# A two-block network on one Trainium2 core: first operand without its root mean square, filter spectrum beside the first product, modulation products moved later

## The chip, the cores and the metric

One core of a Trainium2 chip runs the whole program in one launch. The metric is device time in microseconds (us) for one execution; lower is better. Engines: PE (TensorE), DVE (VectorE), ACT (ScalarE), POOL (GpSimd), and SP, whose queue issues the weight transfers.

## The reference

Two blocks on x (256 rows of 2048 numbers), all in f32. What matters here, cut:

```python
h = rms_norm(x, norm_mix_g)           # x * rsqrt(mean(x*x) + eps) * g
u = h @ w_in                          # 2048 -> 2576 (SSD) + 3520 (RWKV)
x = x + concat([ssd_mixer(u[:, :2576]), rwkv7_mixer(u[:, 2576:])]) @ w_out
x = x + memory_cross_attention(rms_norm(x, g), rms_norm(mem, g), wq, wk, wv, wo)
x = x + square(relu(rms_norm(x, g) @ ffn_w1)) @ ffn_w2
# second block
mod = silu(c) @ ada_w + ada_b         # 2048 -> 12288: shift, scale, gate, twice
mod_c = silu(c_ctx) @ ada_w + ada_b
h, hc = modulate(rmsnorm(x, norm1_g), sh1, sc1), modulate(rmsnorm(ctx, norm1_g), csh1, csc1)
q, k, v, f, hy = split(h @ w_in_2);  kc, vc = split(hc @ w_in_2[:, 1024:3072])
y = merge_groups(attention(q, k, v, kc, vc), fourier_mix(f), hyena_mix(hy, filter_spectrum))
x = x + g1 * (y @ w_out_2)
x = x + g2 * conv_gated_mlp(modulate(rmsnorm(x, norm2_g), sh2, sc2))
return rmsnorm(x, final_norm_g)
```

The filter spectrum is computed from small weights alone (two layers with sine, a third layer, a window, a Fourier transform). The modulation `mod` needs only c, c_ctx and ada_w.

## The kernel before

Activations lie by features: 16 tiles of 128 features by 256 positions. Each weight product is near-f32: a weight chunk of 512 KB lands in one of six buffers (`wraw`), ACT copies it to rounded form (`split_hi`, line 516, tile `whi`), DVE subtracts to get the rest (`split_lo`, line 523, `wlo`); there are four buffers of each. The operand is split in the same way (HH, HL). Each chunk of `gemm_p` is 24 matmuls (lines 566, 568, 569): high by high, high by low, low by high.

The program runs products in a written order: ada0, in_ssd, in_rwkv, xk, xv, out, xq, xo, four times up and dn, ada3, then those of the second block. Every engine walks the same list by itself. SP issues the chunks in that order (`sync`, line 2484), a chunk at a time, each after its buffer is free: a split chunk's buffer is free after `split_lo`, an ada chunk's only after its matmuls on PE. ACT splits three chunks ahead of PE, DVE two.

Beside a product lies other work, cut into steps. `Side.beside(product, every)` lets one step of the side follow each product chunk, more or fewer by `every`; the side's waits stand in the engine's own order, so PE stands still at a side step whose input is late. `weave` puts two steps of an extra product after every `per` steps of the main one.

The modulation product is 24 pieces of 512 columns (`ada_p`, line 692: 16 f32 matmuls in four groups at four column positions of the array; `gather`, line 676, adds the four partial sums; ACT copies PSUM to `mo`, DVE adds the bias into MOD). A piece is 8 chunks, not split. Pieces 0 to 5 are ada0, at the start of the program; 6 to 11 are ada1, woven into xk and xv; pieces 12 and later come in the second block.

Beside ada0 run, one after another: the norm of x (squares on ACT, sums on POOL, matmuls with ones at line 794, square root, reciprocal, x times g and 1/rms on DVE at line 833, high and low split), then the filters' spectrum (lines 930 to 1005), which ends with a store to DRAM that POOL issues and waits for. in_ssd starts after the last MOD of ada0. Its tiles are copied out of PSUM by ACT, with Silu for the first eight (line 1010), those of in_rwkv too (line 1023). Beside in_rwkv runs the SSD mixer, first 12 steps of convolution on DVE (lines 1034, 1037), and later the norm of mem, whose 1/rms is applied after the products xk and xv. Beside xk and xv, and on into out, runs the RWKV mixer, in two halves.

Of the kernel before, what the change touches and what calls it, by code (L numbers as in the profile page):

```python
# [17 lines left out]
NA0 = 6  # L18
WK = 2
WV = 4  # L20
# [3 lines left out]
NA1 = 9  # L24
# [120 lines left out]
def idle(n):  # L145
    for _ in range(n):
        yield
# [39 lines left out]
def build(nc, A_, out):  # L187
    top = ExitStack()
    with top:
# [6 lines left out]
        def landing(name):  # L196
            return count(name, 16)
# [32 lines left out]

        sx, new = scope()
        X0 = new("x0", [P, 16, T])
        TM1 = new("tm1", [P, 8, T])
        RS1 = new("rs1", [P, T])
        sp, new = scope()
        SPEC0 = new("spec", [P, 2, 2, 2, 512])
# [6 lines left out]
        HF = new("hf", [P, 2, 2048])  # L243
        HD = new("hd", [64, 3, T])
        sp.close()
        sx.close()

        rk, new = scope("right")
        RK = new("rk", [P, 28, T + 1])
        sb, new = scope()  # L250
        ZZ = new("zz", [P, 8, T])
        XB = new("xb", [P, 12, T + 3])
        DT = new("dt", [16, 4, T])
# [54 lines left out]
        SMX = new("sm4", [P, 8, 4])  # L308
        s5, new = scope()
# [83 lines left out]
        d_pk, d_mt, d_x0, d_m1, d_sel = (landing(n) for n in ("pk", "mt", "x0", "m1", "sel"))  # L393
# [49 lines left out]
        made(plan_ada("ada0", 0, NA0))  # L443
        made(plan("in_ssd", "w_in", 0, 16, cols(0, 2560) + [(2560, 128)], "a"))
        made(plan("in_rwkv", "w_in", 0, 16, cols(2576, 5648, 256) + [(5648, 224), (5840, 256)], "a"))
        woven = plan_ada("ada1", NA0, NA2)
# [5 lines left out]
        made(plan("xo", "xattn_wo", 0, 16, cols(0, 2048, 256), "v", 2))  # L452
        for i in range(4):
            made(plan(f"up{i}", "ffn_w1", 0, 16, cols(2048 * i, 2048 * i + 2048, 256), "v"))
            made(plan(f"dn{i}", "ffn_w2", 16 * i, 16, cols(0, 2048, 256), "v"))
# [213 lines left out]
        def ada_bank(n):  # L669
            return (1 if NA0 <= n < NA2 else 0) + 2 * (n % 2)  # L670

# [172 lines left out]
        def mem_a(e):  # L844
            e.wait_ge(*d_mem.at("all"))
            e.activation(TM2[:, 0:4, :], MX[:, 0:4, :], ACT.Square).then_inc(*mem.a.up(("sq", 0)))
            yield
            for g in range(1, 4):
                if g > 1:
                    e.wait_ge(*mem.g.at("sum", g - 1))  # L850
                e.activation(TM2[:, 4:8, :], MX[:, 4 * g:4 * g + 4, :], ACT.Square).then_inc(*mem.a.up(("sq", g)))
                yield
                yield
            e.wait_ge(*mem.p.at("ss"))
            e.activation(RS2, PSUM[:, 4, 0:T], ACT.Sqrt, bias=col("eps6"), scale=1.0 / 2048)
            e.activation(RC2[:, :], PSUM[:, 5, 0:4], ACT.Sqrt, bias=col("eps6"), scale=1.0 / 2048).then_inc(*mem.a.up("rt"))
            yield

        def mem_g(e):
            for g in range(1, 4):  # L860
                e.wait_ge(*mem.a.at("sq", g))
                if g > 1:
                    e.wait_ge(*mem.g.now())
                e.tensor_tensor(TM2[:, 0:4, :], TM2[:, 0:4, :], TM2[:, 4:8, :], ADD).then_inc(*mem.g.up(("sum", g)))

        def mem_p(e):
            yield from idle(7)
            e.wait_ge(*ssd.a.end())
            e.wait_ge(*ssd.v.end())
            e.wait_ge(*mem.g.at("sum", 3))  # L870
            for i in range(4):
                e.matmul(PSUM[:, 4, 0:T], ones, TM2[:, i, :], start=i == 0, stop=i == 3)
            for r in range(2):
                for i in range(4):
                    x = e.matmul(PSUM[:, 5, 2 * r:2 * r + 2], TM2[:, i, 128 * r:128 * r + 128], ones[:, 0:2], start=i == 0, stop=i == 3)
            x.then_inc(*mem.p.up("ss"))
            yield

        def mem_v(e):
            yield from idle(7)  # L880
            e.wait_ge(*mem.a.at("rt"))
            e.reciprocal(RS2, RS2)
            e.reciprocal(RC2[:, :], RC2[:, :]).then_inc(*mem.v.up("rs"))
            yield
# [14 lines left out]
        def spectrum_g(e):  # L899
# [6 lines left out]
            yield  # L906
            yield
            yield
            for n in range(4):
                yield  # L910
            for o in range(2):
# [3 lines left out]
                yield  # L915
                yield
                yield
# [92 lines left out]
        def ssd_evac_a(e, g, q, t, what):  # L1010
            e.wait_ge(*mm.at("tile", g, q))
            ps = tile_of(g, q)
            if t < 8:
                x = e.activation(ZZ[:, t, :], ps, ACT.Silu)
            elif t < 20:
                x = e.activation(XB[:, t - 8, 3:T + 3], ps, ACT.Copy)
            else:
                x = e.activation(DT[:, 0, :], ps[0:16, :], ACT.Copy)
            x.then_inc(*ev_a.up((what, g), ("ssd", t)))

        def rwkv_evac_a(e, g, q, t, what):
            e.wait_ge(*mm.at("tile", g, q))
            e.activation(U(t), tile_of(g, q), ACT.Copy).then_inc(*ev_a.up((what, g), ("rwkv", t)))
# [3 lines left out]
        def ssd_v(e):  # L1027
            e.wait_ge(*ev_a.at("ssd", 20))
# [82 lines left out]
            e.wait_ge(*ssd.v.now())  # L1111
            e.tensor_tensor(YS[:, :, :], YS[:, :, :], ZZ[:, :, :], MUL).then_inc(*ssd.v.up("gated"))
# [10 lines left out]
        def ssd_a(e):  # L1123
# [41 lines left out]
            for g in range(2):  # L1165
# [5 lines left out]
                yield  # L1171

# [139 lines left out]
        def mixing_g(e):  # L1312
            e.tensor_tensor(M1C[:, 1:10, 0:64], M1C[:, 1:10, 0:64], M1C[:, 1:10, 64:128], ADD).then_inc(*rw.g.up())
            e.tensor_tensor(M1C[:, 0, 0:64], ident[:, 0:64], ident[:, 64:128], ADD).then_inc(*rw.g.up("masks"))
            for n in range(14):
                e.wait_ge(*ev_a.at("rwkv", 2 * n + 1))
# [1173 lines left out]
        def tensor(e):  # L2490
            e.wait_ge(*d_mt.at("all"))
            side = Side(idle(5), norm_p(e, fn, TM1), spectrum_p(e))
            side.beside(ada_p(e, "ada0", MO0[:, :]))
            side.rest()
            first = lambda e, k: e.wait_ge(*fn.v.at("lo", k // 4))
            e.wait_ge(*ada.v.at("mod", NA0 - 1))
            for _ in gemm_p(e, PL["in_ssd"], [(HH, HL)], first):
                pass
            e.wait_ge(*spt.a.end())
            side = Side(ssd_p(e), idle(1), mem_p(e), idle(12))  # L2500
# [9 lines left out]
            e.wait_ge(*ada.v.at("mod", NA2 - 1))  # L2510
# [15 lines left out]
            side = Side(idle(6), norm_p(e, ctx, TM, lambda e: e.wait_ge(*res.a.at("rt", "xo"))))  # L2526
            for i in range(4):
                side.beside(gemm_wide_p(e, PL[f"up{i}"], GX, lambda e, k: None if i else e.wait_ge(*res.v.at("lo", "xo", k)),
                                        (lambda e, ci: ci == 3 and factor_p(e, "xo", ACC[:, :])) if i == 0 else None))
                side.beside(gemm_wide_p(e, PL[f"dn{i}"], HX, lambda e, k: e.wait_ge(*ff1.v.at("lo", i, k))))  # L2530
# [49 lines left out]
        def vector(e):  # L2580
            ada_first_v(e)
            lo_to = Ahead(split_lo)
            side = Side(idle(5), norm_v(e, fn, X0, TM1, RS1[:, :], HH, HL, lambda j: col("norm_mix_g", j), None), spectrum_v(e))
            side.beside(ada_v(e, "ada0", lo_to))
# [435 lines left out]
```

## Time and profile before

| what | value |
|---|---|
| median of three runs (lowest, highest) | 3333.25 us (3332.19, 3339.2) |
| the profiled execution: its time, its span | 3332.07 us, 3330.2 us |
| mean granted PE clock | 0.965 |
| PE busy, share of span | 3135.5 us, 94% |
| DVE busy | 1870.8 us, 56% |
| ACT busy | 1403.3 us, 42% |
| POOL busy | 240.3 us, 7% |
| HBM read | 591.34 MB, 180 GB/s over the span |

Times in the rows are us from the start of the span unless marked ns. A number in brackets behind a row is the time for which its engine stood idle just before, and what ended that. A granted clock of 1.00 is 2.4 GHz on PE, 0.5 is 1.2 GHz. f32 matmuls appear as two records each.

### The profile page before, as it was taken

How to read it: one execution, taken by the hardware profiler on the slowest of the kernel's cores; microseconds unless marked ns; L12 is line 12 of the kernel's file. 1: busy time of each engine (PE TensorE's matmuls, PEld its weight loads, DVE VectorE, ACT ScalarE, POOL GpSimd, SP SyncE). 2: the span in 40 equal slices, each digit the busy share in tenths (PEclk: the TensorE clock that was granted, in tenths of full speed). 3: DMA queues.
4: the chain of work that ended last, by engine and by line, in shares of the span. 5: the costliest groups of instructions: out<-in, count | busy, mean ns of one | idle time of the engine just before them, and what ended most of it. 6: DMA issues, size and time to landing. Idle time of an engine off the chain costs nothing.

```text
span 3330.2 us, 53960 instructions
## 1 busy us (share of the span) xinstructions
PE 3135.5 (94%) x22542; PEld 2708.2 (81%) x22542; DVE 1870.8 (56%) x2505; ACT 1403.3 (42%) x1992; POOL 240.3 (7%) x204
## 2 busy tenths in 40 slices
PE   6799998989999999999999989999888999999998
PEld 1599897879788888888888769988466888888887
DVE  2247575373655676665656632254445666666666
ACT  1245352253443465444545432344234544445443
POOL 1000122011000110000000300010001000000002
PEclk7899999999999999999999979999988999999999
DMA  8665454555654566565656562445856566656654
GB/s 297 222 177 159 133 179 164 182 168 163 225 161 131 157 203 197 183 194 181 195 185 189 172 203 89 124 143 164 283 177 219 181 185 190 188 176 195 192 178 143
DMA packets 518452, 603.26 MB, mean 181 GB/s; under 512 B 18890, under 2 KB 442981, under 8 KB 516720
## 3 DMA queue, kind: packets, MB, share of 16 engines
q1 hardware_dynamic: 510112, 569.73, 54.6%
q0 software_dynamic: 3488, 25.88, 2.1%
q10 hardware_dynamic: 4608, 4.20, 0.4%
q8 instruction: 178, 2.92, 0.4%
q14 instruction: 66, 0.54, 0.1%
HBM read 591.34 MB, written 8.39 MB: 180 GB/s over the span
## 4 chain that ended last, share of the span: by engine, by line
PE 76%; DVE 4%; issue 4%; DMA 2%; ACT 2%; POOL 1%; SPq 0%; DVEq 0%; ACTq 0%; POOLq 0%
PE psum L594 34%; PE psum L595 18%; PE psum L566 3%; PE psum L568 3%; PE psum L569 3%; PE psum L1725 2%; PE psum L628 2%; PE psum L692 2%; PE psum L631 1%; PE psum L630 1%; DVE wlo L523 1%; PE psum L676 1%; PE psum L2379 1%; DMA wraw<-in_ada_w 1%; PE psum L2137 0%
## 5 line engine op out<-in xcount | busy, mean ns | idle before, releaser
L523 DVE TENSOR_TENSOR wlo<-wraw,whi 128x1024 fp32r<-128x1024 f32 (+2 forms) x916 | 1109.8, 1221 | 561.5 <-ACT whi L516 559.6
L516 ACT ACTIVATE whi<-wraw 128x1024 fp32r<-128x1024 f32 (+2 forms) x916 | 944.8, 1033 | 1078.6 <-PE psum L595 713.2
L594 PE MATMUL psum<-g,whi 128*128 128x512 f32 x2944 | 1045.3, 397 | 1.7 <-DVE wlo L523 1.1
L595 PE MATMUL psum<-g,wlo 128*128 128x256 f32 x2944 | 825.6, 280 | 0.0
L594 PE MATMUL psum<-h,whi 128*128 128x512 f32 x2240 | 791.4, 395 | 6.0 <-DVE wlo L523 5.7
L594 PEld LDWEIGHTS psum<-g,whi 128*128 128x128 f32 x2944 | 556.1, 189 | 136.2 <-DVE wlo L523 2.6
L595 PE MATMUL psum<-h,wlo 128*128 128x256 f32 x2240 | 634.8, 283 | 0.0
L595 PEld LDWEIGHTS psum<-g,wlo 128*128 128x128 f32 x2944 | 556.2, 189 | 0.5
L594 PEld LDWEIGHTS psum<-h,whi 128*128 128x128 f32 x2240 | 422.2, 188 | 103.8 <-DVE wlo L523 6.1
L595 PEld LDWEIGHTS psum<-h,wlo 128*128 128x128 f32 x2240 | 422.8, 189 | 0.1
L566 PE MATMUL psum<-h,whi 128*128 128x256 f32 x1040 | 303.6, 292 | 13.3 <-DVE wlo L523 10.8
L568 PE MATMUL psum<-h,whi 128*128 128x256 f32 x1040 | 297.6, 286 | 0.0
L569 PE MATMUL psum<-h,wlo 128*128 128x256 f32 x1040 | 297.3, 286 | 0.0
L566 PEld LDWEIGHTS psum<-h,whi 128*128 128x128 f32 x1040 | 201.2, 193 | 27.0 <-DVE wlo L523 14.2
L568 PEld LDWEIGHTS psum<-h,whi 128*128 128x128 f32 x1040 | 201.4, 194 | 0.4 <-issue 0.2
L569 PEld LDWEIGHTS psum<-h,wlo 128*128 128x128 f32 x1040 | 200.9, 193 | 0.0
L692 PE MATMUL psum<-wraw,sf 128*32 128x512 f32 x768 | 131.7, 776 | 47.2 <-DMA wraw<-in_ada_w 43.1
L566 PE MATMUL psum<-g,whi 128*128 128x256 f32 x512 | 153.5, 300 | 0.4 <-issue 0.4
L569 PE MATMUL psum<-g,wlo 128*128 128x256 f32 x512 | 145.1, 283 | 0.0
L568 PE MATMUL psum<-g,whi 128*128 128x256 f32 x512 | 145.0, 283 | 0.0
L1840 DVE TENSOR_TENSOR xt<-psum,xt 128x256 f32<-128x256 f32 x192 | 81.2, 424 | 112.2 <-PE psum L595 108.9
L1842 DVE SCALAR_TENSOR_TENSOR xt<-psum,mod,xt 128x256 f32<-128x256 f32 x160 | 77.4, 484 | 77.1 <-PE psum L595 72.6
(464 smaller groups left out, 3350.9 us busy)
## 6 DMA issues: line engine op xcount, KB each, us to landing
wraw<-in_ffn_w SPq DMA_DIRECT2D x256, 512.0 KB, 4.5
wraw<-in_ada_w SPq DMA_DIRECT2D x192, 512.0 KB, 5.6
wraw<-in_w_in SPq DMA_DIRECT2D x172, 512.0 KB, 3.8
wraw<-in_ffn_w_up SPq DMA_DIRECT2D x160, 512.0 KB, 4.5
wraw<-in_w_out SPq DMA_DIRECT2D x64, 512.0 KB, 4.8
wraw<-in_ffn_w_down SPq DMA_DIRECT2D x64, 512.0 KB, 4.7
wraw<-in_xattn_wk SPq DMA_DIRECT2D x32, 512.0 KB, 4.6
wraw<-in_xattn_wv SPq DMA_DIRECT2D x32, 512.0 KB, 6.8
```

Of the source, the lines that this page charges most:

```text
L516: e.activation(high(i), view(WRAW[i % NR], i), ACT.Copy).then_inc(*hi.up(i))
L523: e.tensor_tensor(low(i), view(WRAW[i % NR], i), high(i).bitcast(F32), SUB).then_inc(*lo.up(i))
L566: e.matmul(o, w_hi[:, kk, s:s + 128], XH[:, k, :], start=k == 0 and q % 2 == 0, stop=False, skip_group_check=True)
L568: e.matmul(o, w_hi[:, kk, s:s + 128], XL[:, k, :], start=False, stop=False, skip_group_check=True)
L569: x = e.matmul(o, w_lo[:, kk, s:s + 128], XH[:, k, :], start=False, stop=last, skip_group_check=True)
L594: e.matmul(both_of(g, j), w_hi[:, kk, s:s + 128], X[:, k, :], start=k == 0, stop=False, skip_group_check=True)
L595: x = e.matmul(first_of(g, j), w_lo[:, kk, s:s + 128], X[:, k, 0:T], start=False, stop=last, skip_group_check=True)
L628: e.matmul(o, XH[:, k, sl], w_hi[:, kk, 0:n], start=k == 0 and r * n % 512 == 0, stop=False, skip_group_check=True)
L692: x = e.matmul(PSUM[32 * q:32 * q + 32, ada_bank(n), :], SF[:, k:k + 16, :].rearrange("p k m -> p (k m)"), view(WRAW[(i if q > 1 else befo ...
L1725: x = e.matmul(PSUM[64 * c:64 * c + 64, b, out_at(h):out_at(h) + 64], cell(left, c, left_at(h)), cell(right, c, right_at(h)), start=True, ...
L1840: x = e.tensor_tensor(XT[:, t, :], half, XT[:, t, :], ADD)
L1842: x = e.scalar_tensor_tensor(XT[:, t, :], half, scale(t), XT[:, t, :], MUL, ADD)
```

## The change

x is loaded in four parts by ACT's queue. The first operand becomes x times g, split at once as each part lands (`x_high`, `x_low`); the sums of squares run beside in_ssd, and 1/rms (RS1) is multiplied in when a tile leaves PSUM. That move is now DVE's for all 49 tiles of in_ssd and in_rwkv; the eight tiles of the gate get their Silu on ACT afterwards. ada0 as the first product is gone. in_ssd is the first; beside it run the sums and then the spectrum, at half a step for a chunk (RSPEC). Pieces 0 to 7 are woven into xk and xv (two extra chunks after every two main ones in both, WV was 4), pieces 8 to 11 into up2 and dn2 (two after every four, WF). PE waits for the SSD mixer's last readers of PSUM as a step right behind the mixer; it did so seven steps later. The diff, cut to its core:

```diff
-NA0 = 6
+NA0 = 8
-WV = 4
+WV = 2
+WF = 4
+RSPEC = 0.5
-        made(plan_ada("ada0", 0, NA0))
-        made(plan("in_ssd", "w_in", 0, 16, cols(0, 2560) + [(2560, 128)], "a"))
+        made(plan("in_ssd", "w_in", 0, 16, cols(0, 2560) + [(2560, 128)], "v"))
-        woven = plan_ada("ada1", NA0, NA2)
+        woven = plan_ada("ada1", 0, NA0)
...
+        woven = plan_ada("ada2", NA0, NA2)
         for i in range(4):
-            made(plan(f"up{i}", "ffn_w1", 0, 16, cols(2048 * i, 2048 * i + 2048, 256), "v"))
+            made(weave(plan(f"up{i}", "ffn_w1", 0, 16, cols(2048 * i, 2048 * i + 2048, 256), "v"), woven if i == 2 else iter(()), WF))
...
         def ada_first_a(e):
+            for g in range(4):
+                e.dma_start(X0[:, 4 * g:4 * g + 4, :], A_["x"][:, 4 * g:4 * g + 4, :]).then_inc(*d_x0[g].up("all"))
...
+        def x_high(e, g):
+            e.wait_ge(*d_x0[g].at("all"))
+            for j in range(4 * g, 4 * g + 4):
+                x = e.activation(HH[:, j, :], X0[:, j, :], ACT.Copy, scale=col("norm_mix_g", j))
+            x.then_inc(*fn.a.up(("hi", g)))
+
+        def x_low(e, g):
+            e.wait_ge(*fn.a.at("hi", g))
+            for j in range(4 * g, 4 * g + 4):
+                x = e.scalar_tensor_tensor(HL[:, j, :], X0[:, j, :], col("norm_mix_g", j), HH[:, j, :].bitcast(F32), MUL, SUB)
+            x.then_inc(*fn.v.up(("lo", g)))
...
-        def ssd_evac_a(e, g, q, t, what):
+        def ssd_evac_v(e, g, q, t, what):
             e.wait_ge(*mm.at("tile", g, q))
+            if t == 0:
+                e.wait_ge(*fn.v.at("rs"))
             ps = tile_of(g, q)
             if t < 8:
-                x = e.activation(ZZ[:, t, :], ps, ACT.Silu)
+                x = e.tensor_tensor(ZZ[:, t, :], ps, RS1[:, :], MUL)
...
+        def gate_a(e, t):
+            if t < 8:
+                e.wait_ge(*ev_v.at("ssd", t))
+                e.activation(ZZ[:, t, :], ZZ[:, t, :], ACT.Silu).then_inc(*ssd.a.up(("gate", t)))
+
+        def rwkv_evac_v(e, g, q, t, what):
             e.wait_ge(*mm.at("tile", g, q))
-            e.activation(U(t), tile_of(g, q), ACT.Copy).then_inc(*ev_a.up((what, g), ("rwkv", t)))
+            if t == 0:
+                e.wait_ge(*fills.at("zpad"))
+            e.tensor_tensor(U(t), tile_of(g, q), RS1[:, :], MUL).then_inc(*ev_v.up((what, g), ("rwkv", t)))
...
         def tensor(e):
             e.wait_ge(*d_mt.at("all"))
-            side = Side(idle(5), norm_p(e, fn, TM1), spectrum_p(e))
-            side.beside(ada_p(e, "ada0", MO0[:, :]))
+            side = Side(sums_p(e, fn, TM1, False, 0.3), idle(1), spectrum_p(e))
+            side.beside(gemm_p(e, PL["in_ssd"], [(HH, HL)], lambda e, k: e.wait_ge(*fn.v.at("lo", k // 4))), RSPEC)
             side.rest()
-            first = lambda e, k: e.wait_ge(*fn.v.at("lo", k // 4))
-            e.wait_ge(*ada.v.at("mod", NA0 - 1))
-            for _ in gemm_p(e, PL["in_ssd"], [(HH, HL)], first):
-                pass
             e.wait_ge(*spt.a.end())
-            side = Side(ssd_p(e), idle(1), mem_p(e), idle(12))
+            side = Side(ssd_p(e), then(psum_of_ssd_read, e), sums_p(e, mem, TM2, True), idle(12))
...
+            extra = ada_p(e, "ada2", MO4, WA)
             for i in range(4):
...
+                side.beside(weave(gemm_wide_p(e, PL[f"dn{i}"], HX, lambda e, k: e.wait_ge(*ff1.v.at("lo", i, k))),
+                                  extra if i == 2 else iter(()), WF))
+                if i == 2:
+                    made(extra)
...
         def scalar(e):
             ada_first_a(e)
             hi_to = Ahead(split_hi)
...
+            for g in range(4):
+                hi_to(e, min(g, 2))
+                x_high(e, g)
+            side = Side(sums_a(e, fn, X0, TM1, RS1[:, :], None, 0.3), then(fn.ended, e), spectrum_a(e))
+            side.beside(stream(e, hi_to, 3, PL["in_ssd"], None, gate_a), RSPEC)
...
         def gpsimd(e):
             ada_first_g(e)
-            e.dma_start(X0[:, :, :], A_["x"]).then_inc(*d_x0.up("all"))
...
+            load_filters(e)
+            sums_g(e, fn, TM1)
```

VectorE's program is changed in the same way as ScalarE's: two groups of x are split low before in_ssd, two in its first chunks, and `ssd_evac_v` and `rwkv_evac_v` run in its streams. `load_filters` issues the six filter loads, which POOL issued after the norm before.

## Rows read from the trace of the kernel before

**Rows 1.** Windows: busy us by engine (x instructions), PEclk, DMA share, GB/s
```profile
0.00:132.00 132.00, 83.50 (x300) 28.41 (x300) 30.51 (x51) 25.85 (x34) 17.70 (x22) 0.77 0.78 276
140.00:245.00 105.00, 105.00 (x887) 105.00 (x887) 44.27 (x37) 44.11 (x54) 0.00 (x0) 1.00 0.62 176
254.00:288.00 34.00, 32.32 (x270) 31.98 (x269) 32.68 (x61) 17.44 (x27) 0.00 (x0) 1.00 0.57 165
412.00:450.00 38.00, 38.00 (x315) 37.79 (x316) 33.57 (x41) 14.51 (x21) 20.09 (x14) 1.00 0.56 160
1430.00:1475.00 45.00, 45.00 (x259) 39.32 (x258) 27.68 (x38) 23.43 (x35) 0.00 (x0) 1.00 0.64 196
```

**Rows 2.** Timeline of PE, start to first product: start, us, operation, idle before
```profile
12.27 1.93 PE L692 MATMUL psum<-wraw,sf 128*32 128x512 f32 x8 [12.27 <-DMA wraw<-in_ada_w]
29.41 3.72 PE L794 MATMUL psum<-tm,mats 128*128 128x256 f32 x8
66.73 7.19 PE L939 MATMUL psum<-hw,hd 64*128 64x512 f32 x8
98.50 3.68 PE L952 MATMUL psum<-hf,dft 128*128 128x512 f32 x8
130.20 1.87 PE L676 MATMUL psum<-comb,mo 128*128 128x2 f32 x8 [7.18 <-ACT mo L706]
132.32 0.58 PE L566 MATMUL psum<-h,whi 128*128 128x256 f32 x1 [0.26 <-DVE mod L719]
```

**Rows 3.** Groups of PE in the first 132 us: busy us, mean ns, idle before
```profile
L952 PE MATMUL psum<-hf,dft 128*128 128x512 f32 x32 | 17.2, 686 | 4.4 <-DVE hf L984 3.6 <-ACT spec L1005 0.8
L939 PE MATMUL psum<-hw,hd 64*128 64x512 f32 x16 | 14.8, 1087 | 2.0 <-ACT hd L996 2.0
```

**Rows 4.** Timeline of PE: one woven modulation step, and the seam that ends xv
```profile
604.01 1.05 PE L676 MATMUL psum<-comb,mo 128*128 128x2 f32 x8
605.00 1.06 PE L692 MATMUL psum<-wraw,sf 128*32 128x512 f32 x8
605.99 0.39 PE L566 MATMUL psum<-h,whi 128*128 128x256 f32 x1
...
845.60 1.05 PE L676 MATMUL psum<-comb,mo 128*128 128x2 f32 x8 [0.72 <-ACT mo L706]
875.85 0.79 PE L594 MATMUL psum<-h,whi 128*128 128x512 f32 x1 [5.74 <-DVE wlo L523]
```

**Rows 5.** DMA issue of x, first 125 us: KB each, median us to landing
```profile
x<-in_x POOLq DMA_DIRECT2D x1, 2048.0 KB, 8.8
```

**Rows 6.** Timelines of ACT and DVE: durations of the pieces that the change uses
```profile
459.53 1.69 ACT L889 ACTIVATE h<-mem,pk 128x256 fp32r<-128x256 f32 x4
...
459.96 1.22 DVE L523 TENSOR_TENSOR wlo<-wraw,whi 128x1024 fp32r<-128x1024 f32 x1
461.26 1.67 DVE L895 SCALAR_TENSOR_TENSOR h<-mem,pk,h 128x256 fp32r<-128x256 f32 x4
...
850.62 0.42 DVE L1446 TENSOR_TENSOR rs<-psum,rat 128x256 f32<-128x256 f32 x1 [2.63 <-PE psum L1661]
```

**Rows 7.** Timeline of PE: stalls in in_rwkv and in xk
```profile
286.92 0.38 PE L566 MATMUL psum<-h,whi 128*128 128x256 f32 x1 [1.68 <-DVE wlo L523]
...
502.86 0.39 PE L566 MATMUL psum<-h,whi 128*128 128x256 f32 x1 [2.00 <-DVE wlo L523]
511.13 0.39 PE L566 MATMUL psum<-h,whi 128*128 128x256 f32 x1 [1.90 <-DVE wlo L523]
```

**Rows 8.** Waits of ACT in xk, then in xv: total us, times, longest us
```profile
ACT whi L516 <- DMA wraw<-in_xattn_wk: 61.7, 23, 5.9
...
ACT whi L516 <- DMA wraw<-in_xattn_wv: 8.8, 7, 2.6
```

**Rows 9.** Timeline of ACT: a table load between two functions
```profile
494.02 1.28 ACT L1551 ACT_TABLE_LOAD   x1
495.31 1.06 ACT L1551 ACTIVATE rld<-rld 128x1024 f32<-128x1024 f32 x1
```

More of the change, by code:

```diff
@@ L841, in normed_v, with sums_a @@
             yield
[L844 to L847, printed above, removed]
+        def sums_a(e, s, src, tmp, rs, rc=None, weight=None):
+            e.activation(tmp[:, 0:4, :], src[:, 0:4, :], ACT.Square).then_inc(*s.a.up(("sq", 0)))
+            yield weight
             for g in range(1, 4):
                 if g > 1:
[L850 to L857, printed above, removed]
@@ L859, in mem_g @@
-        def mem_g(e):
+                    e.wait_ge(*s.g.at("sum", g - 1))
+                e.activation(tmp[:, 4:8, :], src[:, 4 * g:4 * g + 4, :], ACT.Square).then_inc(*s.a.up(("sq", g)))
+                yield weight
+                yield weight
+            e.wait_ge(*s.p.at("ss"))
+            x = e.activation(rs, PSUM[:, 4, 0:T], ACT.Sqrt, bias=col("eps6"), scale=1.0 / 2048)
+            if rc is not None:
+                x = e.activation(rc, PSUM[:, 5, 0:4], ACT.Sqrt, bias=col("eps6"), scale=1.0 / 2048)
@@ L860, in mem_g, with sums_g @@
+            x.then_inc(*s.a.up("rt"))
+            yield weight
+        def sums_g(e, s, tmp):
             for g in range(1, 4):
-                e.wait_ge(*mem.a.at("sq", g))
+                e.wait_ge(*s.a.at("sq", g))
                 if g > 1:
[L863 to L870, printed above, removed]
-            for i in range(4):
[L872 to L884, printed above, removed]
+                    e.wait_ge(*s.g.now())
+                e.tensor_tensor(tmp[:, 0:4, :], tmp[:, 0:4, :], tmp[:, 4:8, :], ADD).then_inc(*s.g.up(("sum", g)))
+        def sums_p(e, s, tmp, column=False, weight=None):
+            yield from idle(7, weight)
+            e.wait_ge(*s.g.at("sum", 3))
+            for i in range(4):
+                x = e.matmul(PSUM[:, 4, 0:T], ones, tmp[:, i, :], start=i == 0, stop=i == 3)
+            if column:
+                for r in range(2):
+                    for i in range(4):
+                        x = e.matmul(PSUM[:, 5, 2 * r:2 * r + 2], tmp[:, i, 128 * r:128 * r + 128], ones[:, 0:2], start=i == 0, stop=i == 3)
+            x.then_inc(*s.p.up("ss"))
+            yield weight
@@ new lines, in sums_v @@
+        def sums_v(e, s, rs, rc=None, weight=None):
+            yield from idle(7, weight)
+            e.wait_ge(*s.a.at("rt"))
+            x = e.reciprocal(rs, rs)
+            if rc is not None:
+                x = e.reciprocal(rc, rc)
+            x.then_inc(*s.v.up("rs"))
+            yield weight
+        def x_high(e, g):
[3 more added lines that the diff above has]
+            x.then_inc(*fn.a.up(("hi", g)))
@@ L2699, in scalar @@
             hi_to = Ahead(split_hi)
[L2700 to L2702 removed]
+            for g in range(4):
[3 more added lines that the diff above has]
+            side.beside(stream(e, hi_to, 3, PL["in_ssd"], None, gate_a), RSPEC)
             side.rest()
[L2704 removed]
             spt.ended(e)
             e.wait_ge(*d_spec.at("all"))
[L2707 to L2711 removed]
+            side = Side(ssd_a(e), then(ssd.ended, e), then(mem_landed, e), sums_a(e, mem, MX, TM2, RS2, RC2[:, :]), idle(12))
+            side.beside(stream(e, hi_to, 3, PL["in_rwkv"], None, last=lambda e, ci: ci and mem_high(e, ci - 1)), 1.25)
             mem_high(e, 3)
```

127 lines of the change are left out of this document (66 added, 61 removed).

## The prediction

> **What bounds the kernel now.** I read the windows first. PE is busy in all 105 us of 140 to 245 (in_ssd), in all 38 us of 412 to 450, and in all 45 us of a stretch of the feed-forward products [rows 1]. In such a stretch only work on PE, or a stall put into it, moves the end. The first 132 us are another kind: PE works 83.5 of them, at a mean granted clock of 0.77 [rows 1]. Their timeline shows why: the first modulation matmul waits 12.27 us for its weights, and the last gather waits 7.18 us for ACT's copy before in_ssd's first matmul starts at 132.32 [rows 2]. So the question is what of this stretch can be dropped, and what of its PE work comes back in stretches where PE is full.
>
> PE's price for a chunk of in_ssd: 887 matmul records in 105 us [rows 1], 0.118 us each, 24 in a chunk, 2.84 us. In the feed-forward stretch a chunk is 16 matmuls, 259 in 45 us, 2.78 us [rows 1].
>
> **The change part by part.** The sum is made against the profiled execution, 3332.07 us; its span is 3330.2 us, and it lies 1.2 us below the median of the three runs.
>
> 1. *in_ssd first.* Its first matmul now needs pack, matrices, the first quarter of x, the first weight chunk, and then the splits. Before, pack and matrices (0.55 MB), all of x (2) and two chunks (1) had landed, 3.6 MB, when PE began at 12.27 [rows 2], and x took 8.8 us from its issue [rows 5]. Of the same traffic the new start needs 1.55 MB. Were these bytes served first they would be there near 5.3 us (12.27 x 1.55/3.6); as x's other quarters and later chunks run beside them, I take 7.6, an estimate between that and 12.27, nearer the lower end, since the first needs are also the first issued. Behind it stand on one path: ACT's high copy of the chunk, the same shape as a 1.06 us row [rows 9], its four copies of x times g, 1.69, DVE's four differences, 1.67 [rows 6]. First matmul at 12.0, bounds 9.7 and 16.7. Gain: 132.3 - 12.0 = 120.3 us. The first matmuls run at 1.2 GHz in both kernels (0.58 us for the first one [rows 2]), which cancels. After that weights come faster than PE takes them: at the 276 GB/s of the first stretch [rows 1] a chunk takes 1.9 us, against 2.84.
>
> 2. *Spectrum and sums beside in_ssd.* Their PE work is not hidden, it stands between in_ssd's matmuls in a full stretch. A Fourier step of eight records takes 3.68 us at full clock; the third layer's eight took 7.19 for the same columns [rows 2], so it ran at half clock. Priced at full clock, because PE will be busy: four Fourier steps, 4 x 3.65 = 14.6; third layer, half of 14.8 [rows 3], 7.4; sums, half of 3.72 [rows 2], 1.8; the two small layers about 1. Together +24.8. At half clock it would be twice that: the upper bound. ACT's and DVE's share lies beside PE, both being at 44 of 105 us in this stretch [rows 1].
>
> 3. *48 ada chunks moved* (16 into xv, 32 into up2 and dn2). A woven pair of chunks costs PE 0.99 us, from 605.00 to 605.99, a gather another 0.99, from 604.01 to 605.00 [rows 4]. 24 x 0.99 + 6 x 0.99 = +29.7. PE is full in the feed-forward stretch, so nothing of it hides. A new seam at the end of dn2, where the last gather waits for ACT's copy, costs what the seam that ends xv cost, 0.72 [rows 4]: +0.7. The data has room there: six chunks for some 12 us of PE.
>
> 4. *Tiles leave by DVE.* A PSUM tile of 128x256 with a second operand takes DVE 0.42 us [rows 6]; 49 of them make 20.6 us. In in_ssd and most of in_rwkv DVE has room. It has none in the convolutions: 32.68 of 34 us from 254 to 288, and PE stalled for its split at 286.92 [rows 1, 7]. Into that stretch fall the last tile of in_ssd and four of in_rwkv, 5 x 0.42 = 2.1, with the delay they pass on +2.5. Bounds: 0, and 21 tiles x 0.42 = 8.8 if all of in_ssd's were passed on. PE's wait there holds up the product's next chunk, and nothing else. In the later mixing steps a block of four chunks, 11.4 us, gets 0.84 us more of DVE; I take 0, bound 3. ACT loses its copies, but it ends no wait there.
>
> 5. *Waits inside in_ssd.* A side step now blocks a full PE. The first is the sum of squares: ACT reaches its last square behind the early splits, POOL adds it, and by counting chunks that is ready about 1 us after PE stands at the step. The two sine layers run from PE over DVE to ACT and back; at free pace the third layer waited 2.0 us for the end of that chain [rows 3], now two chunks, 5.7 us, lie between steps: 0 to 1 us late. I take +2.5 in all, bounds 0 and 12 (twice the 4.4 and 2.0 us that the two spectrum groups waited before [rows 3], less a little).
>  What ACT's functions cost here is a point of its own. The load of a table took 1.28 us and the next function started at its end [rows 9]. Silu of the gate now falls between the sines, four loads in about four chunks, 5.1 us, on an engine at 44 of 105 us [rows 1]: hidden. The Trainium skill, page "ScalarE: Activation LUTs", section "Step-by-step: what each stage is for", puts a load at about 2.7 us with the drain. By that the four would be 10.8 us, ACT would be at its limit for those chunks, and the sum could lose about 6 us more. The row decides for 1.28.
>
> 6. *xv woven more densely.* With two extra chunks after two main ones, a main chunk's buffer waits for PE to finish an ada chunk. In xk, so woven, ACT waited 61.7 us for weights, in xv 8.8 [rows 8]. PE hardly saw it, but its cushion is thinner: DVE's long reciprocal then cost 2.00 and 1.90 us in xk [rows 7]. I expect half of that new in xv: +2, bounds 0 and 5.
>
> 7. *End of the RWKV mixer.* The 16 more chunks in xv bring its steps on by 16 x 0.15 x 0.92 = 2.2. The stall of 5.74 us at 875.85 [rows 4], where PE has run out of covered chunks while the mixer's last chain ends, should shrink: -2, bounds -5.7 and +2. The wait moved behind the SSD mixer I cost at nothing: the load of mem, behind the same event, holds the next split anyway.
>
> Sum: -120.3 + 24.8 + 29.7 + 0.7 + 2.5 + 2.5 + 2 - 2 = -60.1. Profiled time 3272.0; as a median 3333.25 - 60.1 = 3273.
>
> **The rivals.**
> - *A. The side steps block PE.* Spectrum waits recur at their old size or more and the clock falls behind them: the upper bound of 5 instead of my value, +9.5, and a fifth of the 24.8 at half clock, +5. 3288. For it: chains over three engines. Against: two chunks between steps.
> - *B. DVE becomes the bound in in_rwkv.* The bounds of 4 in full, 8.8 + 3 instead of 2.5: +9.3, and half the rest of the 20.6 us: 3287. For it: 32.68 of 34 us. Against: that stretch is short.
> - *C. More is gained.* Start at 9.7, no early waits, xv's cushion enough, the stall at 875 gone: -2.3 - 2.5 - 2 - 3.7 = -10.5, 3263.
> - *D. The start isn't early.* If the first operand were as late as the norm had it ready, near 50 us, the gain in 1 would be about 82 and not 120: 3311. Against: x's quarters need no norm.
> - *E. Slower.* Woven ada chunks hold buffers until PE has passed them, so that main chunks land late. ACT's wait in xk, 61.7 us for 16 pairs [rows 8], would come in xv (+52.9) and in up2 and dn2 (+61.7), and reach PE in full: +114.6, 3388. It decides from about half of that reaching PE. Against: xk's waits reached PE for a few us only, and in the feed-forward weave the buffer of a main chunk follows a main chunk (four and two repeat in six, the number of buffers).
>
> **How the numbers follow.** Forecast 3273: 0.56, itself from 3266 to 3281. A 0.13, B 0.10, C 0.15, D 0.03, E 0.03. The range reaches over C and to A and B: 3261 to 3292. Measurements of this kernel can tell about 0.2%, 7 us, from no change. All cases but E are faster by more: faster 0.96, same 0.01, slower 0.03.
>
> **What would show it.** First in_ssd matmul near 12 us, and its end near 160 (12 + 119 + 25 + 2.5); PE full from 15 to 160 but for short waits in front of lines 930 and 939; each woven pair in up2 and dn2 about 1.0 us and no idle before it; the stall near 287, now near 195, some 2 us longer; ACT's wait for xv's weights near xk's. A granted clock under 1 in in_ssd, DVE near 100% through in_rwkv, or PE idle in up2 would make the prediction wrong.

## The result

The changed kernel takes 3303.25 us (median; 3293.84 to 3308.36) beside 3334.08 us for the kernel before (3332.19 to 3339.2) on the same chip: a ratio of 0.9902, 95% interval 0.9876 to 0.9928. It is faster by 31 us. The forecast was 3273 with a range up to 3292: the sign was right, the size was not, and the time lies above the range.

The profiled execution of the changed kernel took 3305.73 us with a span of 3303.9, against 3332.07 and 3330.2 before. Both spans can be cut at the same places: the first matmul of in_ssd, its last tile out of PSUM, and for each later product the first issue of its weights on SP. The stages of each kernel come from one profiled execution. Single stages of like code differ between executions by some 3 us (in_rwkv took 193.8 to 196.9 us in the eight kernels below that share it), and smaller differences of a stage are not read.

| stage, us | before | after | difference | prediction |
|---|---|---|---|---|
| until the first in_ssd matmul | 132.3 | 22.0 | -110.3 | -120.3 |
| in_ssd | 121.3 | 149.8 | +28.5 | +24.8, and most of the 2.5 for waits |
| in_rwkv | 191.3 | 196.6 | +5.3 | +2.5 |
| xk | 209.0 | 206.7 | -2.3 | 0 |
| xv | 171.0 | 207.5 | +36.5 | +9.9 and +2 |
| out | 108.3 | 102.1 | -6.2 | -2 |
| xq, xo | 229.7 | 226.6 | -3.1 | 0 |
| up0 to dn3, ada3 | 772.2 | 794.9 | +22.7 | +19.8 and +0.7 |
| second block | 1395.1 | 1397.7 | +2.6 | 0 |
| span | 3330.2 | 3303.9 | -26.3 | -60.1 |

Some 10 us of the missing 34 are in the start and some 20 in xv and out.

SP issues a chunk up to six chunks ahead of PE, and where two of every four chunks are extras, fewer of those six are main chunks. So the cuts between xk, xv and out don't lie at the same work in two kernels with different weaves. PE's own first matmul of each product does. Those of xk, xv and out, first in the kernel before, then in the changed kernel:

```profile
466.56 0.58 PE L566 MATMUL psum<-h,whi 128*128 128x256 f32 x1 [2.33 <-ACT h L889]
665.09 0.39 PE L628 MATMUL psum<-whi,h 128*128 128x256 f32 x1
846.91 0.50 PE L594 MATMUL psum<-h,whi 128*128 128x512 f32 x1 [0.26 <-DVE mod L719]
```

```profile
389.42 0.39 PE L568 MATMUL psum<-h,whi 128*128 128x256 f32 x1 [1.79 <-ACT h L910]
586.25 0.39 PE L630 MATMUL psum<-whi,h 128*128 128x256 f32 x1
798.73 0.80 PE L596 MATMUL psum<-h,whi 128*128 128x512 f32 x1 [0.26 <-DVE mod L723]
```

By these, xk took 198.5 and 196.8 us, xv 181.8 and 212.5, and from out's first matmul to the first issue of w_q it was 86.3 and 85.9. The growth of xv and out, 30.3 us by the table, lies in xv alone.

The start in the changed kernel, timelines of ACT, POOL, DVE and PE (start, us, operation, idle before):

```profile
17.52 1.06 ACT L518 ACTIVATE whi<-wraw 128x1024 fp32r<-128x1024 f32 x1 [11.15 <-DMA wraw<-in_w_in]
18.49 1.69 ACT L895 ACTIVATE h<-x,pk 128x256 fp32r<-128x256 f32 x4
...
1.29 0.71 POOL L921 DMA_DIRECT2D zt<-in_zt  x1 [0.43 <-issue]
...
4.12 0.59 POOL L926 DMA_DIRECT2D dft<-in_dft  x1
...
20.21 1.67 DVE L901 SCALAR_TENSOR_TENSOR h<-x,pk,h 128x256 fp32r<-128x256 f32 x4 [0.37 <-ACT h L895]
...
22.03 0.55 PE L568 MATMUL psum<-h,whi 128*128 128x256 f32 x1 [22.03 <-DVE h L901]
```

From the split on, the path is the one foreseen: 17.52, the copy, x times g, the difference, 22.03, which is 4.5 us for a predicted 4.4. What is late is the first weight chunk, at 17.5 and not at 7.6. POOL's six loads of the filters (first and last shown) now stand at the head of the program. The DMA groups of the first 60 us (KB each, median us to landing), then the first weight chunk alone, issued at 1.66, and the spread of x's four quarters:

```profile
x<-in_x ACTq DMA_DIRECT2D x4, 512.0 KB, 10.9
win<-in_win POOLq DMA_DIRECT2D x1, 1024.0 KB, 14.5
hw<-in_hy_w POOLq DMA_DIRECT2D x1, 512.0 KB, 10.6
dft<-in_dft POOLq DMA_DIRECT2D x1, 512.0 KB, 16.2
...
wraw<-in_w_in SPq DMA_DIRECT2D x1, 512.0 KB, 15.8
...
DMA to landing us min/median/max: 5.5/10.9/17.2
```

2.1 MB of filters share the engines with 2 MB of x and the weights. The first quarter of x, issued at 0.75, was there after 5.5 us, near what the prediction took. The first weight chunk took 15.8 us, and x's last quarter 17.2, where all of x took 8.8 [rows 5].

The middle, in windows of the changed kernel (columns as in rows 1): in_ssd, then xv and out together, from the first issue of xv's weights to that of w_q.

```profile
22.00:170.00 148.00, 145.47 (x1055) 130.87 (x1056) 85.66 (x99) 63.27 (x82) 16.01 (x10) 1.00 0.56 174
...
575.07:884.64 309.57, 282.21 (x3341) 242.51 (x3342) 166.40 (x178) 123.51 (x173) 36.52 (x30) 0.95 0.58 194
```

And xv and out of the kernel before, between the same two issues:

```profile
653.89:933.17 279.28, 260.31 (x3261) 233.75 (x3262) 168.79 (x176) 121.84 (x171) 36.68 (x30) 0.98 0.56 185
```

in_ssd is full: 145.47 of 148 us, clock 1.00. In xv and out PE's idle time went from 19.0 us to 27.4, and its busy time grew by 21.9, of which the added modulation products explain about 10. The granted clock fell from 0.98 to 0.95. ACT's waits in xv of the changed kernel, and PE's stalls there, from its timeline:

```profile
ACT whi L518 <- DMA wraw<-in_xattn_wv: 74.0, 25, 8.4
```

```profile
598.70 0.39 PE L630 MATMUL psum<-whi,h 128*128 128x256 f32 x1 [2.03 <-DVE wlo L525]
...
599.64 0.42 PE L630 MATMUL psum<-whi,h 128*128 128x256 f32 x1
599.85 0.41 PE L632 MATMUL psum<-whi,h 128*128 128x256 f32 x1
...
620.84 3.78 PE L1665 MATMUL psum<-rla,mats 128*128 128x256 f32 x8 [3.50 <-ACT rla L1572]
...
642.76 2.87 PE L1675 MATMUL psum<-rk,mats 128*128 128x256 f32 x8 [3.40 <-ACT rk L1592]
```

The wait for xv's weights rose from 16.9 to 74.0 us. (The 8.8 of rows 8 was read from a stretch that leaves out the wait of 8.1 us for xv's first chunk.) Behind the stall of 2.03 us PE starts its matmuls 0.21 us apart, which is 1.2 GHz, and does so until 602.8; at full clock they are 0.12 apart. The mixer's steps at 620.84 and 642.76 wait for ACT, whose own order of work also holds the splits.

### The profile page after: what moved, and what is told of

Read it like the earlier page. It is cut to its first block, busy times and chain, and to the rows that moved or that the text cites. A ratio compares the mean times of both kernels' runs of the same rounds, so it can differ in the third digit from the quotient of the medians.

```text
span 3303.9 us, 53982 instructions
## 1 busy us (share of the span) xinstructions
PE 3117.0 (94%) x22542; PEld 2700.3 (82%) x22542; DVE 1882.2 (57%) x2550; ACT 1390.1 (42%) x1962; POOL 240.2 (7%) x203
## 4 chain that ended last, share of the span: by engine, by line
PE 75%; DVE 4%; issue 3%; ACT 2%; DMA 2%; POOL 1%; ACTq 0%; SPq 0%; POOLq 0%; DVEq 0%
PE psum L596 34%; PE psum L597 18%; PE psum L568 3%; PE psum L570 3%; PE psum L571 3%; PE psum L696 2%; PE psum L1754 2%; PE psum L630 2%; PE psum L632 2%; PE psum L633 2%; DVE wlo L525 1%; PE psum L680 1%; PE psum L2408 1%; PE psum L2166 0%; PE psum L1940 0%
## 5 line engine op out<-in xcount | busy, mean ns | idle before, releaser
L696 PE MATMUL psum<-wraw,sf 128*32 128x512 f32 x768 | 123.1, 722 | 21.1 <-DMA wraw<-in_ada_w 17.6
```

What stands on the lines that cost most here:

```text
L696: x = e.matmul(PSUM[32 * q:32 * q + 32, ada_bank(n), :], SF[:, k:k + 16, :].rearrange("p k m -> p (k m)"), view(WRAW[(i if q > 1 else befo ...
```

## The experiments

My theory after the comparison: (1) the filters' loads hold up the first weights; (2) in xv the woven modulation chunks keep their buffers until PE is past them, the splits run late, and PE both stalls and loses clock. The rivals to (2): the mixer's steps come too fast now, since each woven chunk drives them on; the added 16 chunks are simply more traffic; or it is the work of PE itself. Unless told otherwise, an experiment is the changed kernel with the edit shown.

**late_filters.** The filters' loads stand behind the sums on POOL, where they can't meet the first weights.

```diff
-            load_filters(e)
             sums_g(e, fn, TM1)
+            load_filters(e)
```

> The changed kernel with POOL's six filter loads (2.1 MB) issued after the sums of x instead of before. Theory (the filter loads share the first 20 us of transfers with x and the first weight chunks, which POOL issued only after the norm in the kernel before, and which the prediction overlooked): first matmul of in_ssd from 22.0 us to about 12 to 14, the whole 8 to 10 us faster than the changed kernel, in_ssd itself as long as before (about 150 us). Rival (four transfers of x on ACT's queue are slow by themselves, x landed 10.9 us after issue): first matmul stays at 20 or later and the time is the same.

Measured: 3293.78 us (3289.39 to 3296.32), ratio 0.9877 (0.9861 to 0.9894). The first rows of ACT and PE:

```profile
11.14 1.06 ACT L518 ACTIVATE whi<-wraw 128x1024 fp32r<-128x1024 f32 x1 [4.82 <-DMA wraw<-in_w_in]
...
15.64 0.55 PE L568 MATMUL psum<-h,whi 128*128 128x256 f32 x1 [15.64 <-DVE h L901]
```

The start gains 6.4 us, a little less than expected (15.6 for 12 to 14), and the median 9.5, the two spreads overlapping a little. in_ssd keeps its length, 148.9 us, so the spectrum's data is not missed. The filters' loads are the cause of two thirds of the late start. The rest, from 12.0 to 15.6, stays with x's own four quarters and the first chunks: by the mean DMA rates from the start (300 and 282 GB/s) some 3.3 MB had been moved when the split began at 11.14, and some 5 MB at 17.5 in the changed kernel, where I had counted on 1.55.

**no_hold.** The woven modulation pieces 4 to 7, all those in xv, are not loaded and hold no buffer; PE makes the same matmuls on another tile, so those pieces' results are left out.

```diff
-                    PL[name][-1][1].append(chunk("ada_w_2", 0, k, 2, 512 * n, 512))
-                    plain.add(len(chunks) - 1)
+                    if 4 <= n < 8:
+                        PL[name][-1][1].append((None, k, 2))
+                    else:
+                        PL[name][-1][1].append(chunk("ada_w_2", 0, k, 2, 512 * n, 512))
+                        plain.add(len(chunks) - 1)
```

> The changed kernel, but the weights of modulation pieces 4 to 7 (32 chunks, all of xv's extras) are left out: they are neither loaded nor do they take a buffer; PE does the same matmuls on a tile that lies in SBUF, and the side steps fall in the same places. From the issue of xv's first chunk to w_out's first the changed kernel takes 207.5 us, the kernel before 171.0; 11.6 of the 36.5 is PE's work for the 16 chunks more. Theory (buffers held until PE has passed them make the main chunks late, ACT stands at the late split and its mixer steps behind it are late too): the stage falls to 180 to 186 us, ACT's wait for xv's weights from 74 us to under 10. Rival (the mixer's side steps come at other places between the chunks, so PE meets each chain at a worse time): stage stays at 203 us or more though ACT's wait is gone.

Measured: 3274.05 us (3271.79 to 3277.18), ratio 0.9823 (0.9809 to 0.9838), 29 us below the changed kernel. Its window of xv and out, between the same two issues, and ACT's wait in xv:

```profile
571.97:851.34 279.37, 267.56 (x3341) 234.44 (x3342) 166.12 (x178) 122.12 (x173) 36.14 (x30) 1.00 0.48 155
```

```profile
ACT whi L521 <- DMA wraw<-in_xattn_wv: 8.4, 2, 8.0
```

SP runs ahead by six buffers, so the cut between xv and out lies elsewhere here (by it xv takes 151.7 us, below the 180 to 186 of the expectation); the two are read as one. By PE's first matmuls (583.11 and 767.88) xv takes 184.8 us. xv and out take 279.4 us, against 309.6 in the changed kernel and 279.3 in the one before. PE's idle time falls from 27.4 to 11.8 us, and its busy time from 282.2 to 267.6 with the same 3341 records of matmuls, at a clock of 1.00 and not 0.95. So what the loaded chunks cost beyond PE's own work is about 30 us, half of it stalls and half lost clock. What this kernel leaves out is both the holding and the traffic.

**tiny_loads.** The chunks are held as in the changed kernel, but only 64 of each chunk's 512 columns are loaded (the rest of the weights of pieces 4 to 7 is left out): the traffic goes, the holding stays.

```diff
+                    if 4 <= n < 8:
+                        i = len(chunks) - 1
+                        small.add(i)
+                        chunks[i] = (A_["ada_w_2"][k * P:(k + 2) * P, 512 * n:512 * n + 64].rearrange("(k p) n -> p k n", p=P), 2, 512)
...
+                e.dma_start(into[:, :, 0:64] if i in small else into, chunks[i][0]).then_inc(*w_in[i % NR].up())
```

> The changed kernel, but of the weights of pieces 4 to 7 (xv's 32 extras) only 64 of each 512 columns are loaded, the rest is left out: their traffic falls to an eighth, while their buffers are held, and PE's matmuls stand, as in the changed kernel. Theory (the held buffer, not the traffic, makes main chunks late): xv and out together stay at 300 us or more (309.5 in the changed kernel) and ACT's wait for xv's weights stays above 60 us. Rival (the transfers themselves are too many): together 280 to 288 us, as without these chunks.

Measured: 3301.2 us, one time, beside 3332.6. xv and out take 307.5 us, and ACT still waits:

```profile
ACT whi L522 <- DMA wraw<-in_xattn_wv: 81.0, 23, 11.5
```

With an eighth of these chunks' bytes (in xv and out the DMA engines moved 147 GB/s for 194) nothing is won that one run could tell. Traffic is out; with no_hold, holding is what remains.

**before_wv2.** The kernel before, with only the weave changed: four pieces at the start, eight woven at the new density.

```diff
-NA0 = 6
+NA0 = 4
-WV = 4
+WV = 2
```

> The kernel before with only the weave changed: pieces 0 to 3 first, pieces 4 to 11 woven into xk and xv, two extras after every two main chunks in both. If the dense weave alone costs, whichever way, xv grows from 171.0 to 200 to 210 us and out shrinks by some 6, as in the changed kernel. If the growth needs another part of the change (tiles leaving by DVE, the early part), xv takes about 183 us, the 11.6 us of PE's work more. The first stretch, to in_ssd's first matmul at 132.3, gets shorter by 5 to 20 us, held by the spectrum's chain to about 110.

Measured: 3338.6 us, one time, beside 3334.2. The start shrinks by 23.5 us (the first in_ssd matmul comes at 108.8), xv grows from 171.0 to 208.8 and xv and out together from 279.3 to 307.4. So 28 of the 30 us of xv and out come with the weave alone, without any other part of the change; this move by itself gains nothing.

**wa_same.** The woven chunks drive the mixer on by less each, so that it has the pace it had before.

```diff
-WA = 0.15
+WA1 = 0.1125
```

> The changed kernel, but each extra chunk in xk and xv counts 0.1125 of a side step instead of 0.15, so that the 64 extras bring the mixer on by as much as the 48 did before (7.2 x 0.92). Theory of held buffers: xv stays within 5 us of 207.5 us. Rival of side steps at bad places: xv falls to 190 or less, and the stages together (xk to the first w_q chunk, 516.2 us) by 10 or more.

Measured: 3290.84 us, one time. The sum of xk, xv and out is 507.4 us against 516.3; xv 202.9 against 207.5, xv and out 305.7 against 309.6; ACT's wait for xv's weights is 84.8. The expectation of the theory holds narrowly, and the sum fell by 8.8 us where the rival wanted 10. The mixer's pace may be worth up to some 9 us, which one run can't tell from the spread, and not the 30.

**rwkv_act.** in_rwkv's tiles leave PSUM by ACT, as before, without 1/rms, which is left out there.

```diff
-            e.tensor_tensor(U(t), tile_of(g, q), RS1[:, :], MUL).then_inc(*ev_v.up((what, g), ("rwkv", t)))
+            e.activation(U(t), tile_of(g, q), ACT.Copy).then_inc(*ev_a.up((what, g), ("rwkv", t)))
```

> The changed kernel, but in_rwkv's 28 tiles leave PSUM by ACT as a plain copy, as in the kernel before; the factor 1/rms is left out for them. If DVE's 0.42 us a tile is what lengthened in_rwkv with the SSD mixer (from the last tile of in_ssd to w_k's first issue 191.3 us before, 196.6 in the changed kernel), it falls back to 191 to 193. If the two waits of PE that the sums of mem and the readers of PSUM brought are the cause, it stays at 195 to 197.

Measured: 3301.57 us, one time. in_rwkv takes 192.5 us for 196.6, near the 191.3 of before. PE's stalls early in in_rwkv, in the changed kernel:

```profile
192.52 0.39 PE L568 MATMUL psum<-h,whi 128*128 128x256 f32 x1 [0.83 <-DVE wlo L525]
202.08 0.39 PE L568 MATMUL psum<-h,whi 128*128 128x256 f32 x1 [0.51 <-DVE wlo L525]
206.86 0.39 PE L568 MATMUL psum<-h,whi 128*128 128x256 f32 x1 [1.67 <-DVE wlo L525]
```

and in rwkv_act:

```profile
205.89 0.39 PE L568 MATMUL psum<-h,whi 128*128 128x256 f32 x1 [1.68 <-DVE wlo L525]
```

The first two are gone and the third stays, as it was at 286.92 [rows 7]. That is 1.3 us of the difference. In the eight kernels in which DVE empties these tiles in_rwkv took 193.8 to 196.9 us, 195.2 on average, so DVE's evacuation costs it 1 to 4 us, some 3; the changed kernel lies near the upper end.

**v_ffn.** If holding is what costs in xv, it should cost in xk too, and in the feed-forward products, where PE showed no stall, it shouldn't. So all 12 pieces go into up0 to dn2, with the late filters; xk and xv carry none. The norm of ctx, which needs pieces of them, moves beside up3, and the mixer's pace is 1.0 for 0.92. Nothing is left out.

```diff
-        made(weave(plan("xk", "xattn_wk", 0, 16, cols(0, 2048, 256), "v"), woven, WK))
-        made(weave(plan("xv", "xattn_wv", 0, 16, cols(0, 2048, 256), "a"), woven, WV))
+        made(plan("xk", "xattn_wk", 0, 16, cols(0, 2048, 256), "v"))
+        made(plan("xv", "xattn_wv", 0, 16, cols(0, 2048, 256), "a"))
-        woven = plan_ada("ada2", NA0, NA2)
+        woven = plan_ada("ada2", 0, NA2)
...
-            made(weave(plan(f"dn{i}", "ffn_w2", 16 * i, 16, cols(0, 2048, 256), "v"), woven if i == 2 else iter(()), WF))
+            made(weave(plan(f"dn{i}", "ffn_w2", 16 * i, 16, cols(0, 2048, 256), "v"), woven if i < 3 else iter(()), WF))
-RW = 0.92
+RW = 1.0
```

> A version for speed: filter loads late, no modulation chunk in xk or xv, all twelve pieces woven into up0 to dn2 (two after every four), the norm of ctx beside up3, one side step of the mixer for each chunk (RW 1.0). By the theory of held buffers xk, xv and out together fall from 513.7 us (late_filters) to 425 to 455, and the feed-forward products grow by 32 pairs of 1.19 us and 8 gathers, 46 us: in all 3258 to 3280 us. If PE's work is all that the extras cost in xk and xv (43 us), the gain there is 43 and the loss 46: no change against late_filters, 3293.

Measured: 3276.28 us (3274.82 to 3279.38), ratio 0.9831 (0.9816 to 0.9845): faster than both kernels. xk, xv and out sum to 444.9 us, against 513.8 in late_filters, and the feed-forward part takes 842.2 for 795.0. Its weight issues on SP, PE's longest stall in these products, and PE's first matmuls of xk, xv and out:

```profile
361.62 143.41 SPq L2511 DMA_DIRECT2D wraw<-in_xattn_wk  x32
510.70 151.87 SPq L2511 DMA_DIRECT2D wraw<-in_xattn_wv  x32
673.05 128.54 SPq L2511 DMA_DIRECT2D wraw<-in_w_out  x32
...
751.22 0.76 PE L594 MATMUL psum<-h,whi 128*128 128x512 f32 x1 [7.14 <-DVE h L1858]
...
382.65 0.39 PE L566 MATMUL psum<-h,whi 128*128 128x256 f32 x1 [1.79 <-ACT h L908]
545.85 0.39 PE L628 MATMUL psum<-whi,h 128*128 128x256 f32 x1
716.27 0.39 PE L594 MATMUL psum<-h,whi 128*128 128x512 f32 x1
```

64 woven chunks (with 8 gathers) cost 68.9 us in xk and xv, and the same chunks 47.2 in the feed-forward products. That is 1.2 us for each pair and gather there, and 1.7 in xk and xv. Part of the 68.9 can be the mixer's new pace: at the old one (v_ffn92, below) it is 58.1, or 1.5 for each.

**v_ffn92 and v_ffn110.** The same kernel with the mixer's pace at 0.92 and at 1.1.

```diff
-RW = 1.0
+RW = 0.92
```

> The version for speed with the mixer's side steps at 0.92 for a chunk instead of 1.0. Fewer steps beside xk and xv, 5 more left for the end. If the rate of the side steps matters little, within 4 us of v_ffn; if PE meets the mixer's chains too early at 1.0, faster by 5 or more; if the end of the mixer is what is short of cover, slower by 5 or more.

> As v_ffn, with the RWKV mixer's steps taken a tenth faster (RW 1.1 for 1.0) in the products over keys and values. If the 7.1 us idle stretch before the last part of `out` in v_ffn (751.22, behind the mixer's last chain) is only the mixer ending too late, it goes or shrinks to under 2 us and xk, xv and out together fall from 444.8 to about 439: 3270 us. If the side steps are bound by their own chains over DVE, ACT and PE, denser steps only move the waits forward into xk and xv: new idle stretches of 3 us and more in front of the mixer's matmuls, the sum stays at 443 to 450, and the time at 3275 to 3282.

Measured: 3284.49 us (3281.54 to 3289.24), ratio 0.9851 (0.9835 to 0.9868), and 3285.23 us (3282.47 to 3289.27), ratio 0.9844 (0.9828 to 0.9860). xk, xv and out sum to 455.7 and 460.0 us, against 444.9 at 1.0. At 0.92 the stall behind the mixer's last chain is 12.6 us (at 760.60), which is the third case of its expectation: the end of the mixer is short of cover. At 1.1 it is still 5.3 us, and others stand in front of the mixer's matmuls:

```profile
387.64 3.78 PE L1651 MATMUL psum<-rtw,rbt 96*128 96x256 f32 x8 [3.80 <-DMA rkt<-in_ra]
...
595.55 3.78 PE L1673 MATMUL psum<-rk,mats 128*128 128x256 f32 x8 [5.43 <-ACT rk L1590]
```

Idle time of PE in these stages is 36.9 us at 1.1, 34.9 at 0.92 and 27.6 at 1.0. My first expectation for 1.1 fell; the second had the mechanism, and the price was larger than it said (460.0 us for 443 to 450). Of the three paces tried 1.0 is the best: denser steps move the waits to an earlier place, sparser ones leave them at the end.

## Why the prediction was too low

1. *in_ssd first: -120.3, measured -110.3.* The chain behind the split was right to 0.1 us. The step that failed is the 7.6 us, "nearer the lower end, since the first needs are also the first issued". The first quarter of x did land early, but the first weight chunk, issued at 1.66, came at 17.5, 9.9 us later than the 7.6, and behind a 512 KB load of POOL's that was issued at 3.04 and landed 10.6 us later. I did not see that the filters' loads, which stood behind the norm on POOL, now come first, one of the very moves that the diff shows; late_filters puts that at 6.4 us. The rest, 3.6, is left for the sharing with x's other quarters and later chunks; no run took them away. The upper bound of 16.7 would have held without the filters. The Trainium skill, page "DMA: Bandwidth & Descriptors", section "Queues, rings and completion order", says that each DMA engine takes packets in turn from the queues that have work. By that rule a chunk gets a share and not the first place, and the 15.8 us of the first weight chunk agree.

2. *Spectrum and sums, +24.8, and (5) waits inside in_ssd, +2.5: measured +28.5.* Right. The third layer and the Fourier steps ran at full clock, and the one wait is in front of the sums. PE's groups and timeline of the changed kernel in in_ssd:

```profile
L967 PE MATMUL psum<-hf,dft 128*128 128x512 f32 x32 | 14.4, 592 | 0.0
L954 PE MATMUL psum<-hw,hd 64*128 64x512 f32 x16 | 7.9, 615 | 0.0
...
40.73 1.56 PE L875 MATMUL psum<-tm,mats 128*128 128x256 f32 x6 [2.50 <-POOL tm L869]
```

 14.4 and 7.9 us stand for my 14.6 and 7.4. The point on ACT's tables was beside the matter. The sine (line 1011) and Silu (line 1041) follow each other without a load between them, so of the four loads only one came. It took 1.28 us, and Silu started at its end:

```profile
52.44 1.28 ACT L1041 ACT_TABLE_LOAD   x1
53.74 0.42 ACT L1041 ACTIVATE zz<-zz 128x256 f32<-128x256 f32 x1
57.15 0.42 ACT L1011 ACTIVATE hd<-hd 64x256 f32<-64x256 f32 x1 [3.00 <-DVE hd L988]
...
58.43 0.40 ACT L1041 ACTIVATE zz<-zz 128x256 f32<-128x256 f32 x1
```

3. *48 chunks moved, 0.99 a pair.* In the feed-forward part the growth is 22.7 us for a predicted 20.5. A pair in the changed kernel:

```profile
1541.30 1.06 PE L696 MATMUL psum<-wraw,sf 128*32 128x512 f32 x8
1542.29 0.50 PE L596 MATMUL psum<-g,whi 128*128 128x512 f32 x1
1542.63 0.28 PE L597 MATMUL psum<-g,wlo 128*128 128x256 f32 x1
1542.75 0.39 PE L596 MATMUL psum<-g,whi 128*128 128x512 f32 x1
```

 The first product matmul behind the pair takes 0.34 us to the next start, where the others take 0.24 (1542.75 to 1542.98). I had read the pair up to the next start and left out that 0.10. With it, 16 pairs and 4 gathers at 1.09 and the seam of 0.72 are 22.5, which leaves 0.2. The seam came as forecast, 0.72 us at 1695.07. Between the start of up0 and the seam, and on to the end of dn3, PE has no other stall above 0.6 us.

4. *Tiles by DVE, +2.5: measured some 3 of in_rwkv's +5.3* (rwkv_act), inside the bounds. The stall near 287 did not grow by 2 us: it came again with 1.67 us (206.86), and two small ones of 1.3 us together came before it. The other 2 us of in_rwkv are within what executions differ by. DVE was busy for 71% of in_rwkv (138.6 of 196 us) after 70% before, and not near 100%.

6. *xv woven more densely: +2, bounds 0 to 5. This is the step that failed most.* xv and out grew by 30.3 us, all of it in xv. Of these PE's own work is 9.9 (some 11 with the 0.10 of point 3); about 20 are left for what I priced at 2. I had the wait right: "ACT's wait for xv's weights near xk's" came as 74.0 beside 61.7. What was wrong is "PE hardly saw it" in xk. I judged that by the two stalls of rows 7, both behind DVE's reciprocal. But xk's own length shows it. By PE's first matmuls xk takes 163.2 us without woven chunks (v_ffn) and 198.5 with 32 in the kernel before. So a pair of chunks, its share of the gathers included, costs 2.2 us in xk and not the 1.2 of its rows (1.4 with the 0.10); that is some 14 us of xk beyond PE's own work. (v_ffn takes 32 of the mixer's steps beside xk and the kernel before 34; by v_ffn92 that is worth some 3 us, and the pair would cost 2.0.) The cost doesn't appear as one stall with the buffer as its releaser. It is spread over stalls, most of them at the mixer's steps, and over matmuls at 1.2 GHz behind some of them: in xv the stalls of 3.50, 3.40 and 2.79 us (620.84, 642.76, 676.69) are gone in no_hold. That the inputs of these steps come late because they stand behind late splits on ACT and DVE is my reading, and no run shows it by itself.

 The trace before the change held a hint: by PE's first matmuls xk took 198.5 us with 16 pairs and xv 181.8 with 8, which is 2.1 us for each pair more. But that would have given 17 of the 31 us of xv. Why xv lost more than xk stays open.

7. *End of the mixer, -2: measured -0.4, which is nothing that can be told.* The stall of 5.74 us at 875.85 [rows 4] is gone, and the longest wait for a split in out is 1.6 us. But a step of the mixer now holds PE for 3.56 us right before out (793.22), and out itself is as long as before. The -6.2 of the table comes from where SP's cut lies.

Of the rivals none was this. A and B were wrong, since side steps blocked PE in in_ssd for 2.5 us only, and DVE stayed a matter of some 3 us. D was nearest in time (3311) for another reason: the operand was not late by tens of us. E had the mechanism: held buffers, and the wait in xv about as it said, which reached PE for some 20 us out of 57 more of wait. It did not act in up2 and dn2: there ACT waited too, with no stall above 0.6 us on PE but the seam.

```profile
ACT whi L518 <- DMA wraw<-in_ffn_w: 104.1, 40, 7.9
```

 That is the longest wait for weights of all, and nothing on PE goes with it; in v_ffn it is 327.2 us at 1.2 us a pair and gather. What differs is both the density (two in six, as against two in four) and the side work with its chains. xv before had the density of two in six together with the mixer, and its 8 pairs cost 11.4 us against v_ffn's xv (181.8 and 170.4), about PE's own work for them. (With no_hold's 184.8 less its 16 pairs' work as the base it would be some 7 us more.) That points to the density, but no run kept the density and took the side work away.

Two things stay open. One is how the cost divides between held buffers as such and the order in which ACT and DVE meet the late splits; a seventh buffer, which might separate them, wasn't tried. The other is 3 us in xq and xo and 2.6 in the second block, which are within what single stages of like code differ by.

## What to carry over

Cost a piece of woven work by the length of a stage that already carries it, against the same stage or a like one without it, and not by its own duration plus the stalls that name it: here a pair with its share of gathers was 1.2 us by its rows and 2.0 to 2.2 by xk's length. Cut such stages at the bounding engine's own work. At SP's issues, which run ahead by six buffers, the same two kernels give 209.0 and 149.1 us for xk, and a pair would seem to cost 3.7. Work that holds a shared buffer until a late reader is through belongs where it can be woven thinly, beside products with little side work; these runs moved both at once. And when a program gets a new start, list every transfer that is issued before its first matmul, those of the other queues too: they take their share of the same engines.

## What the runs showed of the hardware

- A transfer issued first is not served first. With three queues active in the first 17 us, a 512 KB weight chunk issued at 1.66 landed after 15.8 us, behind a load of the same size that was issued at 3.04 on another queue and landed after 10.6. Without the 2.1 MB on POOL's queue the chunk took 9.5 us.
- After a PE stall of about 2 us in xv the matmuls ran at 1.2 GHz for some 3 us, start to start 0.21 us for 0.12 (599.4 to 602.8). Several such stalls in a stage can cost as much again in clock: in xv and out 15.6 us of idle time and 14.6 of slower busy time lie between the changed kernel and no_hold. They need not: in xk of the changed kernel PE stood idle for 18.5 us, with stalls of 3.42 and 5.12 us (433.74, 442.84), at a mean granted clock of 0.99.
- Sine and Silu alternated on ACT with no table load between them, behind a load for Silu (52.44). In the kernel before, where the sine came first (load at 52.57), Silu had a load of its own at 155.05.
- A product matmul right behind a group at four column positions (1542.29) takes 0.10 us longer to the next start.
